# Attention sums laid head by head in PSUM, divided and turned bank by bank within the loop's last steps

## The reference

```python
def mla_attention(...):               # 16 heads, keys of 96, values of 64
    scores = q @ k.T * scale          # causal by chunks
    out = softmax(scores) @ v         # [256, 16 * 64]
    return out @ w_o

def _windowed_gqa(x, w_qkv, sink, w_o, rel_bias):
    logits = jnp.where(valid, scores + bias, NEG_INF)
    probs = jax.nn.softmax(jnp.concatenate([logits, sink_logit], axis=-1), axis=-1)[..., :-1]
    out = jnp.einsum("bnhgqk,bnkhd->bnqhgd", probs, vw)
    return out.reshape(bsz, s, N_HEADS * HEAD_DIM) @ w_o
```

## Time and profile before

| | us |
|---|---|
| median of 3 runs | 2675.2 |
| lowest and highest | 2674.29 and 2680.39 |
| profiled execution, device time | 2677.76 |
| profiled execution, span of the trace | 2676.0 |
| PE busy in it | 2536.5 |
| DVE busy | 1970.0 |
| ACT busy | 1286.9 |
| POOL busy | 743.2 |

### The profile page before, as it was taken

How to read it: one execution, slowest core, us unless ns; L and a number is a source line. 1 busy time by engine, 2 the same in 40 slices (tenths; PEclk the granted TensorE clock), 3 DMA queues, 4 the chain that set the end, 5 groups by cost and what they waited for, 6 DMA issues and landing times.

```text
span 2676.0 us, 44260 instructions
## 1 busy us (share of the span) xinstructions
PE 2536.5 (95%) x14322; PEld 2227.4 (83%) x14322; DVE 1970.0 (74%) x3577; ACT 1286.9 (48%) x1913; POOL 743.2 (28%) x754
## 2 busy tenths in 40 slices
PE   7779997899999999999999999889998999999998
PEld 6679876898889888888888888679897888888887
DVE  5768756687657998567777777568997567777776
ACT  4656546555544155544444444563165444444443
POOL 0300003000000100245555555230101255555554
PEclk9999999999999999999999999989999999999999
DMA  6135641456554423666666665424513666666664
GB/s 194 55 118 182 190 146 55 140 181 190 170 165 153 150 70 92 208 190 190 191 190 189 190 192 183 133 79 158 150 60 108 211 188 189 189 190 193 190 190 146
DMA packets 169935, 424.64 MB, mean 159 GB/s; under 512 B 13373, under 2 KB 65981, under 8 KB 169070
## 3 DMA queue, kind: packets, MB, share of 16 engines
q1 hardware_dynamic: 166832, 418.86, 51.0%
q10 hardware_dynamic: 3006, 4.49, 0.5%
HBM read 420.11 MB, written 3.18 MB: 158 GB/s over the span
## 4 chain that ended last, share of the span: by engine, by line
PE 87%; DVE 7%; ACT 3%; issue 2%; POOL 0%; DVEq 0%; DMA 0%; SPq 0%; POOLq 0%; ACTq 0%
PE PS L459 18%; PE PS L460 18%; PE PS L461 18%; PE PS L692 13%; PE PS L774 8%; PE PS L694 7%; PE PS L802 3%; DVE oh L2054 1%; ACT arena L1031 1%; PE PS L641 1%; PE PS L749 1%; DVE lo L1413 1%; DVE xx L1461 1%; DVE oh L2051 0%; PE PS L621 0%
## 5 line engine op out<-in xcount | busy, mean ns | idle before, releaser
L1413 DVE TENSOR_TENSOR lo<-raw,hi 128x1024 fp32r<-128x1024 f32 x716 | 1061.8, 1507 | 513.7 <-ACT hi L931 511.5
L931 ACT ACTIVATE hi<-raw 128x1024 fp32r<-128x1024 f32 x716 | 747.2, 1052 | 325.5 <-PE PS L461 303.2
L459 PE MATMUL PS<-hi,Ah 128*128 128x512 f32 x1024 | 403.1, 394 | 11.2 <-DVE lo L1413 7.1
L460 PE MATMUL PS<-lo,Ah 128*128 128x512 f32 x1024 | 402.5, 393 | 0.0
L461 PE MATMUL PS<-hi,Al 128*128 128x512 f32 x1024 | 399.8, 390 | 0.0
L692 PE MATMUL PS<-xx,hi 128*128 128x512 f32 x1504 | 371.4, 389 | 0.0
L459 PE MATMUL PS<-xx,hi 128*128 128x256 f32 x1152 | 328.7, 285 | 3.2 <-DVE xx L1461 3.2
L692 PEld LDWEIGHTS PS<-xx,hi 128*128 128x128 f32 x1504 | 282.3, 188 | 58.6
L460 PE MATMUL PS<-xx,hi 128*128 128x256 f32 x1152 | 327.6, 284 | 0.0
L461 PE MATMUL PS<-xx,lo 128*128 128x256 f32 x1152 | 327.5, 284 | 0.0
L1334 ACT ACTIVATE gl<-gl 128x256 f32<-128x256 f32 x188 | 78.6, 418 | 481.1 <-DVE gl L2097 481.1
(11 more groups left out here) (241 smaller groups left out, 3566.1 us busy)
## 6 DMA issues: line engine op xcount, KB each, us to landing
raw<-in_peer_u SPq DMA_DIRECT2D x256, 512.0 KB, 3.6
raw<-in_peer_v SPq DMA_DIRECT2D x256, 512.0 KB, 4.4
raw<-in_ffn_w_up SPq DMA_DIRECT2D x88, 512.0 KB, 3.7
raw<-in_ffn_w_down SPq DMA_DIRECT2D x44, 512.0 KB, 4.2
raw<-in_peer_w_q SPq DMA_DIRECT2D x32, 512.0 KB, 4.5
raw<-in_da_w_qkv SPq DMA_DIRECT2D x24, 512.0 KB, 4.1
raw<-in_conv_w_in SPq DMA_DIRECT2D x24, 512.0 KB, 3.9
raw<-in_attn_w_qkv SPq DMA_DIRECT2D x12, 512.0 KB, 4.0
```

The lines of the kernel that those rows point to most:

```text
L459: pe.matmul(o, ah, bh, start=start, stop=False)
L460: pe.matmul(o, ah, bl, start=False, stop=False)
L931: cp.activation(hi[:, s, 0:size], raw[:, s, 0:size], ACT.Copy).then_inc(hi_made, 1)
L1413: V.tensor_tensor(lo[:, s, 0:size], raw[:, s, 0:size], hi[:, s, 0:size].bitcast(F32), ALU.subtract).then_inc(lo_made, 1)
```

## The change

In `mla` and `gqa` alone:

- Piece number q becomes 2 * s + t, so that a bank is full once three and a half heads are done. `sums_in` is as it was.
- DVE's division is cut into a function `part_out(b)` for one bank: one reciprocal (in `gqa` an addition ahead of it), then a multiply over the heads of which both tiles are in the bank, and one of 64 columns for a head of which only one is. `PARTS_AT` says at which step of DVE's loop banks 0, 1 and 2 are divided: 12, 15 and 19 in `mla`; 18, 18 and 19 in `gqa`. Banks 3 and 4 follow after the loop, with half of the `xl` pieces after each.
- PE turns banks j = 0 and 1 of the result at its step 21, j = 2 at step 22, and j = 3 inside `wide`, ahead of its block kc = 2.
- ACT makes the hi of blocks B, B + 1 and B + 2 at its steps 17, 18 and 19, not after the loop. DVE makes the lo of B and B + 1 at its steps 17 and 18; before, it made that of B after the division, and that of B + 1 after the `xl` pieces.
- DVE's two sink steps of `gqa` move into its loop, at steps 16 and 17.
- The small copy and its semaphore are gone. `mla.O` lies elsewhere, off the query rows.

```diff
-        mla.O = view(1344, TT, D)
+        mla.O = view(4416, TT, D)
...
+        PARTS_AT = {"da": (), "mla": (12, 15, 19), "gqa": (18, 18, 19)}
...
-            q = t * 16 + s
+            q = 2 * s + t
             return q // 7, (q % 7) * 65
...
                 for kc in range(kcs - 2):
+                    if kc in within:
+                        within[kc]()
                     pe.wait_ge(lo_made, made(B + kc))
                     input_ready(kc)
...
+            def turn_heads(a, js, bank):
+
+                ao = S(f"{a.name}_o_read")
+                turn("o" + a.name, lambda t, k: a.O[:, t, k * P:(k + 1) * P], js,
+                     lambda j: [(ao, (8 * j + 7) // 7 + 1)], bank)
...
                     if s >= 7:
                         values(s - 7)
+                    if a is not da and s >= a.nsub + 5:
+                        turn_heads(a, (0, 1) if s == a.nsub + 5 else (2,), bank)
...
-            pe.wait_ge(S("mla_o_made2"), 2)
-            turn("omla", lambda t, k: mla.O[:, t, k * P:(k + 1) * P])
             fresh[0] = xt["omla"][0]
-            wide("mla_wo", xh, xl, KD)
+            wide("mla_wo", xh, xl, KD, {2: lambda: turn_heads(mla, (3,), lambda: 4)})
...
+                    if a is not da and a.nsub < s <= a.nsub + AHEAD:
+                        splits_to(plan[f"{nm}_wo"][0] + s - a.nsub)
...
+                def part_out(b):
+
+                    q, n, o = sums_in(b)
+                    dve.wait_ge(S(f"{nm}_values_made"), (q + n - 1) // 2 + 1)
+                    inv = rden.rearrange("p s t -> p (s t)")
+                    sums = o[:, :, a.e]
+                    if a is gqa:
+                        dve.wait_ge(S("sink_exp"), 1)
+                        link(V.tensor_tensor(den[:, q:q + n], sums, sink_e[:, q:q + n], ALU.add))
+                        sums = den[:, q:q + n]
+                    link(V.reciprocal(inv[:, q:q + n], sums))
...
+                    if a is gqa and s == a.nsub:
+                        dve.wait_ge(S("gqa_max_made"), 2 * GQA_H)
...
+                    if a is gqa and s == a.nsub + 1:
+                        dve.wait_ge(S("sink_tanh"), 1)
...
+                    if a is not da and s in (a.nsub + 1, a.nsub + 2):
+                        splits_to(plan[f"{nm}_wo"][0] + s - a.nsub)
+                    for b, at_s in enumerate(PARTS_AT[nm]):
+                        if at_s == s:
+                            part_out(b)
...
-                dve.wait_ge(S(f"{nm}_o_read"), 5)
-                V.tensor_copy(rstd[:, 4:5], rstd[:, 0:1]).then_inc(S(f"{nm}_o_made2"), 2)
-                splits_to(plan[f"{nm}_wo"][0] + 1)
+                part_out(3)
+                turned("o" + nm, None, 0, range(4))
+                part_out(4)
+                turned("o" + nm, None, 0, range(4, KD))
```

More of the change, by code:

```diff
@@ L511, in paired_group, with wide @@
                 fresh[0] = None
-            def wide(name, ah, al, kcs):
+            def wide(name, ah, al, kcs, within={}):
                 B, G0 = plan[name]
@@ L557, in wide, with turn @@
                     acc_free[G0 + h] = [(x_new, xadds[name] + 3 + h)]
-            def turn(name, src):
+            def turn(name, src, js=None, ready=None, bank=None):
                 base, kcs = xt[name]
-                for j in range((kcs + 1) // 2):
+                for j in range((kcs + 1) // 2) if js is None else js:
                     ks = [k for k in (2 * j, 2 * j + 1) if k < kcs]
-                    b = aux((name, j), [(xt_lo, base + ks[-1] + 1)])
+                    b = aux((name, j), [(xt_lo, base + ks[-1] + 1)], bank() if bank else None)
+                    for s, v in ready(j) if ready else ():
+                        pe.wait_ge(s, v)
                     for k in ks:
@@ L667, in attention @@
                         values(s - 7)
+                    if a is not da and s >= a.nsub + 5:
+                        turn_heads(a, (0, 1) if s == a.nsub + 5 else (2,), bank)
                 ao = S(f"{nm}_o_read")
-                acc_free[groups[-1]] = acc_free[groups[-1] - 1] = [(ao, 2 * DA_H if a is da else 5)]
+                acc_free[groups[-1]] = acc_free[groups[-1] - 1] = [(ao, 2 * DA_H if a is da else 4)]
                 bank_free[4] = [(ao, 2 * DA_H if a is da else 5)]
@@ L910, in _ @@
                     attention(gqa, (G0, G0 + 1))
-                    acc_free[G0 - 2] = acc_free[G0 - 1] = [(S("gqa_o_read"), 5)]
-                    pe.wait_ge(S("gqa_o_made2"), 2)
-                    turn("ogqa", lambda t, k: gqa.O[:, t, k * P:(k + 1) * P])
+                    acc_free[G0 - 2] = acc_free[G0 - 1] = [(S("gqa_o_read"), 4)]
                     fresh[0] = xt["ogqa"][0]
-                    wide("gqa_wo", xh, xl, KD)
+                    wide("gqa_wo", xh, xl, KD, {2: lambda: turn_heads(gqa, (3,), lambda: 4)})
                 norm("n7" if layer else "n5")
@@ L944, in turned @@
                     if k % 2 == 0:
-                        n = aux_at[(name, k // 2)]
-                        act.wait_ge(aux_full, n)
-                        b = 4 + (n - 1) % 4
+                        act.wait_ge(aux_full, aux_at[(name, k // 2)])
+                        b = aux_bank[(name, k // 2)]
                     sc = 1.0 if gain is None else (pT[:, gain + k:gain + k + 1] if isinstance(gain, int) else gain)
@@ L1448, in splits_to, with turned @@
                     nxt[0] += 1
-            def turned(name, gain, first=0):
+            def turned(name, gain, first=0, ks=None):
                 base, kcs = xt[name]
-                for k in range(kcs):
-                    b = 4 + (aux_at[(name, k // 2)] - 1) % 4
+                for k in range(kcs) if ks is None else ks:
+                    b = aux_bank[(name, k // 2)]
                     dve.wait_ge(xt_hi, base + min(k - k % 2 + 2, kcs))
@@ L1639, in head_out @@
                                                da.otmp[:, t, :], ALU.mult, ALU.add).then_inc(S("da_o_read"), 1)
+                def part_out(b):
[8 more added lines that the diff above has]
+                    link(V.reciprocal(inv[:, q:q + n], sums))
+                    heads = a.O.rearrange("p t (h e) -> p h t e", e=a.e)
+                    for x0, x1 in ((q, q + q % 2), (q + q % 2, q + n - (q + n) % 2), (q + n - (q + n) % 2, q + n)):
+                        if x0 == x1:
+                            continue
+                        rows, sum_of = o[:, x0 - q:x1 - q, 0:a.e], inv[:, x0:x1]
+                        if x1 - x0 == 1:
+                            i = V.tensor_tensor(heads[:, x0 // 2, x0 % 2:x0 % 2 + 1, :], rows,
+                                                sum_of.unsqueeze(2).to_broadcast([P, 1, a.e]), ALU.mult)
+                        else:
+                            i = V.tensor_tensor(heads[:, x0 // 2:x1 // 2], rows.rearrange("p (h t) e -> p h t e", t=TT),
+                                                sum_of.rearrange("p (h t) -> p h t", t=TT).unsqueeze(3)
+                                                .to_broadcast([P, (x1 - x0) // 2, TT, a.e]), ALU.mult)
+                    i.then_inc(S(f"{nm}_o_read"), 1)
                 for s in range(a.nsub + (8 if a is da else 4)):
```

30 lines of the change are left out of this document (5 added, 25 removed).

## The result

The changed kernel takes **2690.05 us** in the median of 6 runs (2688.83 to 2690.78), the kernel before 2675.87 beside it (6 runs, 2673.98 to 2680.39). The ratio is 1.0046, with an interval of 1.0035 to 1.0056: 14.2 us slower. The forecast was 2685, 9.6 us slower; the measured time lies at the very end of its range of 2668 to 2690. On another chip the same kernel took 2689.28 beside 2677.40, ratio 1.0045 (1.0032 to 1.0058), 11.9 us slower. The execution profiled took 2690.78, its span 2688.9.

The account below looks back on a forecast made before the run. PE, busy for 95% of the span, was taken as the bound, so time could come only from its idle or low clock. 2.0 + 0.6 + 7.0 = +9.6 us on the median 2675.2 gave 2684.8, said as 2685; range 2668 to 2690.

Parts of the forecast that it names:

- The walk through the loop: End of both loops: splits, wait for ACT and banks delay head 15's pair by 5.0 us in `mla`, 6.6 in `gqa`.
- The clock in the tails: Behind both loops PE's clock is low: projection starts 2.0 us later in `mla`, 0.6 earlier in `gqa`, summed as +0.6.
- the rival with the clock up: Clock stays high through both tails: +2.8 us, 2678; chance 0.22.
- The wait at kc = 2: Inside each projection, PE waits for the lo of B + 2: 3.5 us, idle for 3; twice 7.0 us.
- the clock also falls behind the new wait: Rival, in both projections: low clock behind each 3 us idle, 1.7 us each; +13.0, 2688; chance 0.14.
- the sum with the low tails: Both places, clock low through both tails: 2.0 + 0.6 + 7.0 = +9.6 us.
- The base: Whole kernel: forecast counted from the median of 2675.2, 2.6 us below the profiled execution of 2677.76.
- the work fits in gaps: Rival, DVE's loops: head 15's pair is not delayed, projections start 4.9 and 9.5 us earlier; -8.6, 2667; chance 0.14.

Follow-up runs that it names:

- e2: The changed kernel with DVE's los of B and B + 1 moved out of the loop to behind bank 2; 2677.69 beside 2677.75, ratio 1.0003.
- e3: The kernel before with only DVE's two sink steps moved into its loop at steps 16 and 17; 2673.61 beside 2677.75, ratio 0.9984.
- e8: As e6, with banks 0 to 2 of `gqa` divided behind the pair of head 15; 2663.88 beside 2679.43, ratio 0.9949.
- after: The changed kernel itself, against the kernel before; 2690.05 beside 2675.87, ratio 1.0046.
- e4: The kernel before with its last four transposes ahead of kc = 2 and the los around the last `xl` pieces; 2683.91 beside 2677.75, ratio 1.0024.
- e5: The changed kernel with the edits of e1 and e2 together; 2671.80 beside 2677.40, ratio 0.9979.
- after_again: The changed kernel run once more, unaltered, on a second chip; 2689.28 beside 2677.40, ratio 1.0045.
- e6: As e5, with ACT's hi splits also out of the loop and DVE's lo of B behind bank 3; 2671.32 beside 2677.40, ratio 0.9975.
- e1: The changed kernel with the lo of B + 2 made behind the first four `xl` pieces, ahead of the last bank; 2681.97 beside 2677.75, ratio 1.0016.

## Why the prediction was right, and where its size was off

**The walk through the loop** held. It had the pair of head 15 come 5.0 and 6.6 us later; measured from the points it came 4.7 (42.07 less 37.36) and 6.6 (12.78 less 6.15). The wait of DVE for ACT's hi was there, 1.75 us in `mla` and 1.33 in `gqa`. e2 shows what the delay is made of: without the los it is 0.6 and 2.9, and of the 2.9 the sink steps alone make 0.8 (e3), banks 0 and 1 ahead of the last pair 2.1 (e8).

**The clock in the tails** was the choice that decided between the forecast and the rival with the clock up. It was low, as taken (0.50 in the windows of both). The starts came 1.7 and 0.0 us later, where the sum had 2.0 and 0.6 (its own terms give 0.5). Ahead of the last two heads PE idled for 2.85 and 0.68 us in `mla`, 3.15 and 1.81 in `gqa`. e2 shows the other case in `mla`: with short waits the clock stays at 1.00.

**The wait at kc = 2** came in both places as said: the idle was 2.67 us, said as 3, with the transposes 3.3 of the 3.5. Twice it is 6.5, where the sum had 7.0.

**The term that was mis-sized** is the clock behind that wait. The forecast had none; it stood among the rivals as "the clock also falls behind the new wait", at 1.7 each and with a chance of 0.14. It fell in both places. The spacing of the matmuls there, summed over its excess above 0.2275 us, gives 1.7 and 1.7, just that rival's price. Against it stand 0.4 and 0.6 us less at the projection's start, which now begins at the high clock; the sum with the low tails had no term for that either. So it should have read 1.7 + 0.0 + 6.5 + 3.4 - 1.0 = +10.6, where the ledger has +10.7. The rival's own sum of +13.0 was too high by 0.9 in its tails, 0.5 in its idles and this 1.0. The forecast of +9.6 came so near the ledger partly by luck: it left out 3.4 us and had 2.4 too much elsewhere. I gave the rival too little: an idle of 2.67 us is longer than the 1.63 us that the clock fell behind in `gqa` before, and that row was the very reason for taking the tails as slow.

The rule of the Trainium skill that the prediction drew on (page "TensorE: Matmul & The Clock Gate", section "A second HAM failure mode: psum-queue depth-cycling"), that repeated short idles between groups of matmuls can drive the clock up and down without a long one, agrees with after: in `mla` the granted clock is 0.50 in 475 to 481, 1.00 in 484 to 488, and 0.50 again in 492 to 494, with idles of 2.85 and 2.67 us ahead of the two falls. It doesn't say which of two equal idles does it, and e4 shows that not each does.

**The base.** The rest, 11.9 or 14.2 measured against 9.9 or 10.7 in the ledger, came from stretches that the change doesn't touch. The prediction had no term for them, and no part of the forecast stands for them: against the medians of the first set it is 4.6 us low, of which 3.5 are such stretches and 1.1 the two places.

**The rivals.** That the work fits in gaps fell with the pair of head 15. What it wanted is to be had all the same: e5, the same change but for the place of the los, is 5.6 us faster than before. About 3.6 of its ledger's 7.6 us are what the sink steps gain alone in e3. That the clock stays up in the tails fell too, with a granted clock of 0.50 in both.

What stays open is why the same wait is followed by a fall in some places only (below), and how much of e8's 15.5 us is drift. The ledger holds 11.5; the profiled executions, 2665.51 and 2677.76, differ by 12.2; the median of the kernel before in that set, 2679.43, was the highest of the four.

## What to carry to other kernels

Side work that is moved into a loop's last steps must stand behind the last link of the chain on its engine, not in front of it: two instructions of 1.22 us at each of two places, ahead of the last head, cost 12 us together, since they brought a wait for another engine, the delay itself, and the clock. Where a product is cut into a projection, make every operand that the next block needs ahead of the late piece; one line there was worth 8 us. And where a sum depends on the clock, price each PE idle of a size that already brought it down in the trace as one that may well do so again (five of eight here), at every place, and not as a small chance.

## What the runs showed of the hardware

The same idle of 2.67 us, in front of the same block, was followed by the lower clock in five of eight places: both of after, both of after_again, and `mla` in e2. It was not in `gqa` of e2 and in both of e4. In all five the projection had begun at the high clock (its first matmuls 0.09 to 0.12 us over their usual spacing in all); in the other three the clock had come back only during its first matmuls (0.46 to 1.24 us over). That splits the cases cleanly, but eight places and no run made for it are no proof of a cause. The Trainium skill says in the same page, under "Part 1: The HAM clock gate", that what the gate watches isn't tied to the program's start, so that the count of slow matmuls varies from run to run; against that as the whole cause, the four places of after and after_again, on two chips, fell alike.

A fall at that place took 1.45 to 1.7 us, by the spacing of the matmuls behind it. In the tails of the two loops the shortest idle with a fall behind it was the 1.63 us of before; the idle of 1.89 us in e6 had one too, while waits of up to 0.73 us in `mla` of e2 had none.

The stretch ahead of `mla` moved by as much as 3.2 us between executions (431.21 in e1, 434.38 in e4), with a mean granted clock of 0.98 and 0.96 over it, and the median of the kernel before by 3.6 us between sets of runs. For a question of 2 us, times from a point just ahead of the change told more than the span did.
